# Layer 0 merge, output projection, second norm and query for two latent tiles alone, the other two latent tiles and the two context tiles in fused phases beside the experts

## The reference

```python
g_att, g_sc, g_hy = jnp.split(jax.nn.sigmoid(gate_pre), 3, axis=-1)      # gate_pre = h @ w_in[:, GT0:]
m = g_att * (y_att @ w_att) + g_sc * (y_sc @ w_sc) + g_hy * (y_hy @ w_hy)
x = x + gt1 * (m @ w_o)                                                  # the same for ctx in layer 0
h2 = _rmsnorm(x, g_norm2) * (1.0 + sc2) + sh2
q = (h2 @ wq).reshape(128, 8, 2, 64)                                     # per tile of 128 tokens
s = jnp.einsum('chpd,hpnd->chpn', q, subkeys)
# top 16 of each half, top 16 of their 256 sums: 16 experts e with weights g for each token and head
a = gelu(jnp.einsum('chkd,cd->chk', u_tab[e], h2))
out = jnp.einsum('chk,chkd->cd', g * a, v_tab[e]);  x = x + gt2 * out
```

## Time and profile before

| what | value |
|---|---|
| time, median of 3 runs (lowest, highest) | 5394.02 us (5386.65, 5394.62) |
| span of the profiled execution, first to last instruction | 5406.6 us |
| busy: PE, DVE, ACT, POOL | 3763.2, 3264.4, 1947.0, 1959.6 us |
| moved by DMA | 1532.43 MB, of it 1342.26 MB by gathers |

### The profile page before, as it was taken

The page is one execution under the profiler, slowest core; times in us unless marked ns, Lnnn a source line. Parts: engine busy times, 40 slices in busy tenths (PEclk is TensorE's granted clock), DMA queues, the critical chain, the costliest instruction groups (busy, mean ns, idle before and its releaser), DMA issues. The chain is left out here.

```text
span 5406.6 us, 59650 instructions
## 1 busy us (share of the span) xinstructions
PE 3763.2 (70%) x19504; PEld 1823.9 (34%) x19504; DVE 3264.4 (60%) x7012; ACT 1947.0 (36%) x5112; POOL 1959.6 (36%) x1521
## 2 busy tenths in 40 slices
PE   6899879987555555555497788668976555555554
PEld 3677338876111111111122245246852111111111
DVE  7522452323777777777647778764136777777776
ACT  5432002222434334434334434325223433443443
POOL 5112003322444444444343356212433444444443
PEclk7999889998777777777798889889987777777777
DMA  5011001112999999999999989831328999999998
GB/s 238 16 44 71 4 16 63 62 71 89 399 420 410 414 408 421 413 414 415 391 407 358 361 335 378 348 146 42 100 84 334 421 410 416 410 418 416 410 418 347
DMA packets 230644, 1532.43 MB, mean 283 GB/s; under 512 B 26164, under 2 KB 26740, under 8 KB 58044
## 3 DMA queue, kind: packets, MB, share of 16 engines
q0 software_dynamic: 184320, 1342.26, 60.7%
q1 hardware_dynamic: 46012, 186.36, 9.3%
HBM read 1515.31 MB, written 13.21 MB: 283 GB/s over the span
## 5 line engine op out<-in xcount | busy, mean ns | idle before, releaser
L536 PE MATMUL psum<-arena 64*64 64x512 f32 x10240 | 1752.8, 818 | 1230.9 <-ACT arena L515 1207.1
L491 POOL DMA_INDIRECT arena<-in_uv,arena x1280 | 1446.9, 1130 | 1878.1 <-PE psum L536 1438.7
L651 DVE SCALAR_TENSOR_TENSOR arena<-arena 128x1024 f32<-128x1024 f32 x1280 | 1597.5, 1248 | 736.9 <-DMA arena<-in_uv,arena 681.0
L536 PEld LDWEIGHTS psum<-arena 64*64 64x64 f32 x10240 | 415.4, 168 | 2524.9 <-ACT arena L515 1880.4
L1527 PE MATMUL psum<-view_at,view_at 128*128 128x512 f32 (+1 forms) x4896 | 964.7, 358 | 19.3 <-PEq L165 10.3
L504 ACT ACTIVATE arena<-arena 128x1 f32<-128x1 f32 x1280 | 258.3, 202 | 1865.1 <-DVE arena L651 1794.2
L1527 PEld LDWEIGHTS psum<-view_at,view_at 128*128 128x128 f32 x4896 | 813.9, 191 | 183.7 <-issue 53.3
L265 POOL TENSOR_TENSOR view_at<-view_at,view_at 128x1024 fp32r<-128x1024 f32 (+1 forms) x180 | 398.8, 2225 | 1208.7 <-ACT view_at L299 1207.7
L515 ACT ACTIVATE arena<-arena 128x64 f32<-128x64 f32 x1280 | 445.1, 348 | 75.8 <-PE psum L536 33.9
L508 ACT ACTIVATE arena<-arena 128x1 f32<-128x1 f32 x1280 | 376.8, 294 | 47.1 <-ACT arena L504 0.8
L299 ACT ACTIVATE view_at<-view_at 128x1024 fp32r<-128x1024 f32 (+1 forms) x176 | 164.0, 939 | 327.9 <-DMA view_at<-in_w_in 186.4
(11 more groups left out here) (243 smaller groups left out, 3368.4 us busy)
## 6 DMA issues: line engine op xcount, KB each, us to landing
view_at<-in_w_in SPq DMA_DIRECT2D x108, 512.0 KB, 5.6
view_at<-in_w_mod SPq DMA_DIRECT2D x48, 1024.0 KB, 11.6
arena<-in_uv,arena POOLq DMA_INDIRECT x1280
view_at<-in_w_br SPq DMA_DIRECT2D x48, 256.0 KB
view_at<-in_w_out SPq DMA_DIRECT2D x16, 512.0 KB, 8.7
view_at<-in_wq SPq DMA_DIRECT2D x16, 512.0 KB, 3.3
arena<-mod_rows SPq DMA_DIRECT2D x12, 512.0 KB
keep_spectrum<-arena SPq DMA_DIRECT2D x18, 256.0 KB, 7.3
```

The source lines that it names most:

```text
L491: nc.gpsimd.indirect_dma_start(out=self.slots[i % self.ring], out_offset=None, in_=self.table, in_offset=bass.IndirectOffsetOnAxis(ap=self ...
L536: last = nc.tensor.matmul(self.c.psum[tokens, at:at + 512], self.diag[rows, k % 4], self.slots[k % self.ring][rows, D + h * 512:D + (h + 1 ...
L651: nc.vector.scalar_tensor_tensor(out=self.junk, in0=self.slots[i % self.ring][:, 0:D], scalar=1.0, in1=self.h2_turned if i % 2 else self.h ...
```

## The change

In layer 0 the four phases run for tiles 0 and 1 (256 columns) alone. At the start of `phase_merge`, behind the first four weight loads, SP stores the columns 256 to 767 of h and of the three y in DRAM (`later_h0`, `later_y0_*`). The new `phase_later_beside` does everything from the gates to the scores for two tiles, 256 columns, with a share of the gathers; it runs twice: for tiles 2 and 3 (`LAST_LATENTS`) beside the gathers 0 to 235, and for tiles 4 and 5 (`CONTEXT`) beside the gathers 260 to 491. It loads h and y back, and all weights of the merge, the output projection and the query again, into a ring of three slots scattered over free memory (`ScatteredRing`). Its output projection is turned the other way (weights stationary, then transposes of the result), the sigmoid is made from a tanh, and the keys come one head at a time. The split of weights is on POOL, all other splits on DVE. The tiles' expert sums now all use bank 4. The memset of the score pad in `phase_query` is gone, and the gate row of the context is loaded in the last `phase_experts`. Layer 1 calls the same functions with the sizes that it had.

```diff
@@ phase_merge
-            ring.load(sp, proj)
+            ring.load(sp, proj, range(SLOTS))
+            for dst, src in stores:
+                sp.dma_start(dst, src).then_inc(stored, 16)
+            ring.load(sp, proj, range(SLOTS, n_all))
+            if stores:
+                sp.wait_ge(stored, 16 * len(stores))
...
@@ class Share
-        return self.first + self.n * (s * parts + part + 1) // (self.steps * parts)
+        a, b = self.ends[s:s + 2]
+        return self.first + self.n * (a * parts + (b - a) * (part + 1)) // (self.ends[-1] * parts)
...
+class ScatteredRing:
...
+    def load(self, sp, n, used):
+        block, kt = self.blocks[n]
+        if n >= self.slots:
+            sp.wait_ge(used, n - self.slots + 1)
+        sp.dma_start(self.raw[n % self.slots][:, 0:kt], block).then_inc(self.landed[n % self.slots], 16)
...
+LAST_LATENTS = Later(2, 0, 152, (88, 96), 168, ((176, 180), (189, 193), (197, 132)))
+CONTEXT = Later(4, 1, 168, (96, 80), 136, ((144, 148), (189, 193), (197, 132)))
...
+def later_steps():
+    steps, weights = [("lead", i) for i in range(3)], [4] * 3
+    for g in range(N_GATES):
+        steps += [("gate", 2 * g), ("value", 2 * g + 1)]
+        weights += [4, 2]
+    steps += [("merged", i) for i in range(2)]
+    weights += [1] * 2
+    steps += [("out", N_MERGE + b) for b in range(KD)]
+    weights += [4] * KD
+    steps += [("added", i) for i in range(2)] + [("norm", i) for i in range(6)]
+    weights += [1] * 2 + [2] * 6
+    steps += [("query", N_MERGE + KD + h) for h in range(PH)]
+    weights += [5] * PH
+    steps += [("scored", i) for i in range(2)]
+    weights += [1] * 2
...
+def phase_later_beside(c, layer, where, experts, first, last, h_kept, ys_kept):
...
+        @ph.block.gpsimd
+        def _(pool):
+            for s, (kind, n) in enumerate(steps):
+                share.gpsimd(pool, s)
+                if kind == "lead" and n == 2:
+                    ring.split(pool, 0)
+                if kind in ("gate", "value", "out", "query"):
+                    ring.split(pool, n + 1)
...
+            for s, (kind, n) in enumerate(steps):
+                if kind in ("gate", "value"):
+                    g, kt = n // 2, KD if kind == "gate" else KB_BR
+                    ring.wait(pe, n)
...
+                    feature_job(c, ring.parts(n), bank(n), W, kt, of, after=lambda k: share.tensor(pe, s, k, kt)).then_inc(proj, 1)
...
+                share.tensor(pe, s)
...
+            for s, (kind, n) in enumerate(steps):
+                share.scalar(act, s)
...
+                if kind == "value":
+                    g = n // 2
+                    act.wait_ge(proj, n)
...
+                    nc.scalar.activation(sig[:, g % 2], c.psum[:, bank(n - 1):bank(n - 1) + W], ACT.Tanh, scale=0.5).then_inc(sig_d, 1)
...
+                if kind in ("gate", "value", "out", "query"):
+                    ring.round_one(act, n + 2)
...
@@ build
-        phase_merge(c, 0, lay)
-        phase_out(c, 0, True, lay)
-        phase_norm2(c, 0, True)
-        experts = Experts(c, 0, range(NT), (4, 0, 4, 0, 4, 4))
-        phase_query(c, 0, True, experts)
...
+        phase_merge(c, 0, lay, GROUP_TILES, [(h_kept, c.hT[:, :, later])] + [(ys_kept[br], lay.ys[br][:, :, later]) for br in range(3)])
+        phase_out(c, 0, lay, GROUP_TILES)
+        phase_norm2(c, 0, GROUP_TILES)
+        experts = Experts(c, 0, range(NT), (4, 4, 4, 4, 4, 4))
+        phase_query(c, 0, GROUP_TILES, experts)
...
+        group = GROUP_TILES * experts.per_tile
+        phase_later_beside(c, 0, LAST_LATENTS, experts, 0, group - 20, of([h_kept], 0), of(ys_kept, 0))
+        phase_experts(c, experts, group + 4)
+        phase_later_beside(c, 0, CONTEXT, experts, group + 4, 2 * group - 20, of([h_kept], 1), of(ys_kept, 1))
         latents = NT_LAT * experts.per_tile + 8
-        phase_experts(c, experts, latents)
+        phase_experts(c, experts, latents, [(experts.gates[:, 1], spread_row(c, 0, GT2, 1))])
```

More of the change, by code:

```diff
@@ L36 @@
 NT = NT_LAT + NT_CTX
+GROUP_TILES = 2
+GROUP_W = GROUP_TILES * P
 GRID_W = 64
@@ L283, in __init__, with load @@
         self.high_ready, self.ready = ph.sem("w_high_ready"), ph.sem("w_split")
-    def load(self, sp, used):
-        for n in range(self.ahead, len(self.blocks)):
+    def load(self, sp, used, blocks=None):
+        for n in range(self.ahead, len(self.blocks)) if blocks is None else blocks:
             block, kt = self.blocks[n]
@@ L333, in parts, with __init__, round_one, split @@
         return self.high[:, n % self.slots], self.low[:, n % self.slots]
+class ScatteredRing:
+    def __init__(self, c, ph, blocks, places):
+        self.c, self.blocks, self.slots = c, blocks, len(places)
+        self.raw = [c.own(raw, KD, P) for raw, _ in places]
+        self.low = [c.rounded(raw, KD, P) for raw, _ in places]
+        self.high = [c.rounded(high, KD, P) for _, high in places]
+        self.landed = [ph.sem(f"w_landed{s}") for s in range(self.slots)]
+        self.high_ready, self.ready = ph.sem("w_high_ready"), ph.sem("w_split")
+    def load(self, sp, n, used):
[3 more added lines that the diff above has]
+        sp.dma_start(self.raw[n % self.slots][:, 0:kt], block).then_inc(self.landed[n % self.slots], 16)
+    def round_one(self, act, n):
+        if n < len(self.blocks):
+            s, kt = n % self.slots, self.blocks[n][1]
+            act.wait_ge(self.landed[s], 16 * (n // self.slots + 1))
+            self.c.nc.scalar.activation(self.high[s][:, 0:kt], self.raw[s][:, 0:kt], ACT.Copy).then_inc(self.high_ready, 1)
+    def split(self, pool, n):
+        if n < len(self.blocks):
+            s, kt = n % self.slots, self.blocks[n][1]
+            pool.wait_ge(self.high_ready, n + 1)
+            split(self.c.nc, self.c.nc.gpsimd, self.high[s][:, 0:kt], self.low[s][:, 0:kt],
+                  self.raw[s][:, 0:kt]).then_inc(self.ready, 1)
+    def wait(self, pe, n):
+        pe.wait_ge(self.ready, n + 1)
+    def parts(self, n):
+        return self.high[n % self.slots], self.low[n % self.slots]
 class Mixing:
@@ L664, with __init__ @@
 class Share:
-    def __init__(self, experts=None, first=0, last=0, steps=1):
-        self.experts, self.first, self.n, self.steps = experts, first, last - first, steps
+    def __init__(self, experts=None, first=0, last=0, steps=1, weights=None):
+        self.experts, self.first, self.n = experts, first, last - first
+        self.ends = [0] + list(itertools.accumulate(weights or [1] * steps))
     def place(self, s, part=0, parts=1):
-        return self.first + self.n * (s * parts + part + 1) // (self.steps * parts)
+        a, b = self.ends[s:s + 2]
+        return self.first + self.n * (a * parts + (b - a) * (part + 1)) // (self.ends[-1] * parts)
     def tensor(self, pe, s, part=0, parts=1):
@@ L2471, in query_blocks, with phase_norm2 @@
     return [(c.io["wq"][layer][h], KD) for h in range(PH)]
-def phase_norm2(c, layer, full):
+def phase_norm2(c, layer, nt):
     nc = c.nc
-    tiles = list(range(NT if full else NT_LAT))
+    tiles = list(range(nt))
     h2N = c.at(80, NT, D)
```

315 lines of the change are left out of this document (293 added, 22 removed).

## The result

The changed kernel takes 5326.8 us, median of 4 runs (5323.6 to 5332.5), against 5393.5 us for the kernel before, median of 4 (5386.7 to 5394.6): a ratio of 0.9879, 95% interval [0.9865, 0.9893], 67 us or 1.2% faster. The profiled spans are 5321.6 and 5406.6 us.

A forecast was written before the change was run, and what follows sets the result against it. It took PE to bound the sequential half, with idle DMA engines, and DMA to bound the gathers. Terms: -268 + 218 + 4 + 28 + 15 = -3 us, so 5391 us; range 5335 to 5450 with rivals.

The forecast's parts named there:

- What the sequential part gives back: Layer 0's merge, output projection, norm and query ahead of the first gather: 268 us less (250 to 290).
- What the fused phases add: Loads beside layer 0's gathers: 64.0 MB at 3.4 us for 1 MB, 218 us more, plus 4 for 1 KB rows.
- the third leg: Price evidence from a merge with nothing beside: 49.5 us for 16 MB, 3.1 us for 1 MB.
- have made the gathers later: Beside POOL's gathers, SP's loads delay gathers rather than fill a gap: 367 GB/s while the share stayed at 0.95.
- some 70 us faster: Whole change by the skill page's bytes / 436e3 us, an estimated 147 us for the fused phases' 64 MB.
- the mixed stretches above measured half as much again: Reason for setting aside the page's 147 us: stretches with gathers and other transfers gave 3.2 and 3.4 us for 1 MB.
- Idle DMA time and ends: Fused phases: 2% idle DMA time, 28 us (0 to 84); three more phase ends in the gathers, 15 us (9 to 25).
- The waiting in line: Fused phases: ACT, PE and POOL wait with work queued behind, waits of 2 to 5 us; taken as 2%, 28 us.
- Edits at nothing: Tanh, missing memset, context's gate row and all sums in bank 4: hidden by gathers; uncovered, the bank would cost 16 us.
- Loads as cheap as gathers: Faster rival, fused phases: loads at 2.42 us for 1 MB, 155 us; full effect 5296, half granted, 5344 us; chance 0.25.
- The slower rival: Fused phases run like the stretch at 3150, DMA idle 6%, 84 instead of 28 us: 5447 us; chance 0.30.
- The sign of being wrong: The prediction is wrong if a fused phase takes under 660 or over 750 us.

The follow-up runs named there:

- e8: Changed kernel with the merge's stores spread in pieces, six weight slots instead of four there, lead-step weights 7 instead of 4: 0.9831 of the kernel before.
- e1: Kernel before plus 122 unused loads of 512 KB in 4 KB rows (64 MB) beside layer 0's gathers: 5556.5 us against 5405.6, 1.0275.
- e2: Kernel before plus 122 unused loads of 512 KB in 1 KB rows beside layer 0's gathers: 5584.9 us, 1.0334.
- e14: Kernel before with six slots for gathers instead of eight, no weights added: 1.0807 of the kernel before.
- e13: Kernel before with POOL's split of a weight block one job later in layer 1's projections beside the gathers: 0.9976.
- e4: Kernel before with the expert sums of all six tiles of layer 0 in bank 4, nothing else: 0.9996.
- e9: Changed kernel with only the context pair fused; the latent pair runs the four phases ahead of the experts: 5321.3 us, 0.9852 of the kernel before.
- e12: e8 with the first y's rounding one lead step later on ACT and its split behind the first gate's sums on DVE: 0.9826 of the kernel before.
- e15: Kernel before with five slots for gathers instead of eight, about two under way, no weights added: 1.1782 of the kernel before.

## Why the prediction was wrong, by its own steps

- **What the sequential part gives back: right.** Merge 142.8 us for 144, output 42.4 for 42, norm 22.2 for 23, first gather 36.1 us into the query phase for 35; together 270.3 for 268. The way of the weights, not PE, set the merge, at 5.17 us a gate for 5.2; with six slots for the weights it fell to 4.32 (e8).
- **What the fused phases add: the step that failed.** "I take 3.4, 109 us for a group, 218 us more", and 4 for the rows of 1 KB: 222 us. By e1 and e2 it is 56.7 MB x 2.36 + 7.3 MB x 2.8 = 154 us, 68 too many. The step under it is "they would take 149 us alone. The DMA engines were busy 0.95/1.01 of 200 us = 188 us, so 39 us went into 12.1 MB": it takes the share as time that the bytes needed, and charges all of the surplus to the loads. e14 shows the same share and rate with no such bytes, e13 takes the shortfall away with the bytes in place and brings the same formula to 2.5 us. The merge's 0.20 for 64 GB/s, the third leg, is farther still from a saturated stretch; no run tests it by itself. The sentence that SP's loads "have made the gathers later" rests on the same stretch; there it was POOL's wait that made them late.
- **The weighing of the page against the rows.** The Trainium skill, DMA: Bandwidth & Descriptors, "Anatomy of one DMA", gave an estimated 147 us for the 64 MB and "some 70 us faster". The section has the figure for the gpsimd path; these loads are issued by SP, and the measured 151 us of e1 agree within 3%. For rows of 1 KB it is too low: 179 us in e2. That the measured 67 us agree with the whole is partly luck, since the spans differ by 85. I set it aside for "the mixed stretches above measured half as much again"; they had measured waiting. Its section "Issuing engines are not separate DMA queues" holds as well: 417 GB/s for both kinds together (e1), 415 for gathers alone.
- **Idle DMA time and ends: about right.** 28 + 15 = 43 us forecast; 186.7 - 154 = 33 left over by the measured prices, of which the start of the first group alone is some 11. The two terms were not measured apart. The waiting in line was the right mechanism, but its place was the lead steps, where ACT stood before `h`, not the value steps: from 1150 to 1700 and in the second phase the DMA engines are at 1.00.
- **Edits at nothing: right for the bank** (e4). The tanh, the memset and the gate row were not run by themselves; the sum leaves no room for a large cost of theirs.
- **The rivals.** "Loads as cheap as gathers" was right, with the sign that I gave it for ("421 GB/s beside loads of 1 MB each"), and its price of 155 us for the loads is the 154 of e1 and e2. I gave it 0.25, and with the half of its effect that I granted it, 5344, it still came out 17 us too slow. The slower rival, a fused phase like the stretch at 3150, did not come. The sign of being wrong that I had set, a fused phase under 660 or over 750 us, did not show it either: at 677.2 and 673.6 us both phases lie inside, so that sign was too wide for a range of 115 us.
- **The sum with the one term put right:** -268 + 154 + 28 + 15 = -71, 5323 us; measured 5326.8. The closeness is partly luck. The terms are read from spans, and the span fell by 85 us while the median fell by 67, as the profiled execution before was 12.6 us over its median and the one after 5 under. On the spans the sum is 14 us short, most of it in the idle time and the ends.

What stays open: why the context's stretch is 8 us longer behind a fused latent group than in e9, and how the remaining 33 us divide between idle time and ends. e12 shows only that a fuller start does not bring time back.

## What to carry to other kernels

Take the price of added DMA traffic from a stretch in which the DMA engines are full (bytes over GB/s at a share of 1.0), not from one below it: there the busy share held waiting as well, and looked like dear bytes. If only such a stretch is at hand, read the share by queue before a price is charged to one kind of transfer. When a mixed stretch runs below the full rate, look for what keeps the issuing engine from its next transfer, here POOL's split one job too early behind ACT's rounding, and move that first. And cost each moved part by itself, its saving too: of two like groups one paid for the whole change, and the other broke even, as long as the merge had four slots for its weights.

## What the hardware showed unasked

- 8, 6 and 5 slots for gathers of 1 MB give 415, 365 and 318 GB/s; the share reads 1.01, 0.96 and 0.87. The time of the gathers' queue over the whole kernel is 3282, 3517 and 3630 us for the same 1342 MB (before, e14, e15).
- Beside saturated gathers, direct loads in rows of 4 KB cost 2.36 us for 1 MB, in rows of 1 KB 2.8, stores in rows of 2 KB 2.3, and the sum of both kinds stays at 411 to 422 GB/s. The gathers' own queue took 3282 and 3283 us before and after.
- Cutting 5.2 MB of stores into pieces of 256 KB between the loads gained 3 us, where no load had been issued for 13.6 us.
